# Sums of squares in a two-block fp32 kernel: four squares added by GpSimd, a reordered first product, a held PSUM bank

## The chip, the cores and the metric

The kernel runs on one core of one Trainium2 chip. The metric is the device time of one execution in microseconds, lower is better; where several executions are named, it is their median. TensorE multiplies, VectorE and ScalarE work elementwise, GpSimd is a further, slower elementwise engine, SyncE issues most of the loads.

## The reference

Activations are 512 tokens by 1024 features. Two transformer layers come first (the "first block"), then one layer of a second model (the "second block"), which also has a context stream of 256 tokens.

```python
def layer_norm(x, g, b):
    mu = jnp.mean(x, axis=-1, keepdims=True)
    var = jnp.mean(jnp.square(x - mu), axis=-1, keepdims=True)
    return (x - mu) * lax.rsqrt(var + LN_EPS) * g + b

def hybrid_layer(x, ...):                       # twice
    proj = x @ w_in                             # three kinds of attention on slices of proj
    h = layer_norm(ALPHA * x + heads @ w_o, ln1_g, ln1_b)
    ffn = (silu(h @ w_gate) * (h @ w_up)) @ w_down
    return layer_norm(ALPHA * h + ffn, ln2_g, ln2_b)

def second_block(x, c, ctx, c_ctx, ...):
    mods = split(silu(c) @ w_mod + b_mod, 9)    # and the same of c_ctx
    h = x + 0.5 * g1 * swiglu(rmsnorm(x, norm_ffn1) * (1 + sc1) + sh1, ...)
    hc = ctx + 0.5 * g1c * swiglu(rmsnorm(ctx, norm_ffn1) * (1 + sc1c) + sh1c, ...)
    ...                                         # retention, convolution, a second swiglu
```

## The kernel before, in words

Activations lie transposed, features on the 128 partitions: eight tiles of 128 features by 512 tokens, `X[:, c, :]`. Products keep fp32 accuracy by splitting: each operand is a high part and a low part, and each block product is three matmuls, high by high, high weight by low operand, low weight by high operand (`mm3`, L726 to L728). Weights come as panels of up to 16 blocks of 128 by 128, in the order of use, through two buffers (`wraw`, `whi`, `wlo`): ScalarE copies the high part (L1105), VectorE subtracts the low part (L1549), and `prep` of a panel stands in each engine's own program, mostly one panel ahead of its use (`at`). `panel` makes TensorE wait for the low part of a panel, and `two` runs a panel's tiles over all k, waiting per k for the operand's low part (`ready`), which comes after its high part.

Each engine has its own hand-ordered program, and the programs meet by semaphores. Rings hand out buffers: the PSUM banks are shared among the rings `PB` (0 to 3), `OB` (4 to 7), `AB` (0 to 6) and `ZB` (7). `take` gives the bank that was least recently handed out, whoever still reads it; the new user then waits for that reader. `hold` keeps a bank from being handed out until `give`.

A LayerNorm of the first block runs so. GpSimd adds tiles 0 to 5 of X (`add_up`, L2124), TensorE sums that and tiles 6 and 7 over the features by products with a matrix of ones (`total`, through `sum_of`, L798; each of its products is two records of the trace). VectorE subtracts the mean tile by tile (`center`, L1602, event `mid`). ScalarE squares each centred tile (`square`, L1135) into a ring of three buffers in `tmp_a` (`SQA`), and TensorE sums the eight squares by eight more products (`squares`). ScalarE turns the sum to 1/sqrt by Ln and Exp (`rstd`, L1127, L1129), then per tile VectorE scales (L1591), ScalarE adds the bias and gives the high part (`emit`, L1162), and VectorE the low part (L1572). Then the next products start: `gu f0` or `f1` after ln1, `qkB` of layer 1 after ln2 of layer 0. After ln2 of layer 1 comes the first RMS norm of the second block, rms1, whose squares ScalarE makes as it adds the LayerNorm's bias (L1361).

Between these sums TensorE makes the 36 tiles of modulation (c @ w_mod) by small products, at places written by hand (`mod_point`): "make" (L783, 16 records with 32 columns of weights), "row", a copy by ScalarE (L1117), and "turn" (L789, 4 records of two columns), which VectorE reads out (L1561). At rms1 TensorE runs the context's gate tile 0, the squares, the context's gate tile 1, the modulation, and then the x stream's gate tiles.

## Time and profile before

| | us |
|---|---|
| median of 3 executions | 3098.67 |
| lowest, highest | 3096.65, 3101.64 |
| profiled execution | 3101.29 |
| its span in the trace | 3099.5 |
| TensorE busy in the span | 3045.9 (98%) |
| VectorE, ScalarE, GpSimd busy | 1500.5, 1025.6, 277.8 |
| TensorE's mean granted clock | 0.995 |

Busy times are sums over the instructions of one engine. A matmul's duration in the trace is longer than the distance to the next one, since they are pipelined, so the distances count. Times in the rows are microseconds from the span's start. The granted clock is given as a share of 2.4 GHz; 0.50 is 1.2 GHz.

### The profile page before, as it was taken

The numbers are of one execution on the slowest core, as the hardware profiler recorded it, in microseconds if no ns is written. First come the engines' busy times: TensorE is split into PE (matmuls) and PEld (weight loads), VectorE is DVE, ScalarE is ACT, GpSimd is POOL, SyncE is SP. The second block draws the span as 40 slices with busy tenths as digits, with TensorE's granted clock in tenths as the row PEclk, the third lists the DMA queues.
The fourth block names the chain that finished last, engine by engine and source line by source line (L and its number), as shares of the span: only waits on it lengthen the run. The fifth ranks groups of instructions, "written<-read, shape, count | busy, mean of one in ns | idle before, by whom it ended". The sixth has DMA issues, their size and how long they took to land.

```text
span 3099.5 us, 35135 instructions
## 1 busy us (share of the span) xinstructions
PE 3045.9 (98%) x14888; PEld 2449.3 (79%) x14888; DVE 1500.5 (48%) x2261; ACT 1025.6 (33%) x1533; POOL 277.8 (9%) x210
## 2 busy tenths in 40 slices
PE   8999999999999999999999999999999999999998
PEld 6756778877667888878888888788888887878887
DVE  4565333344665334352323234576868694443333
ACT  4543222234543223242121123443333335232222
POOL 0232000001323000000000001010101021000000
PEclk9999999999999999999999999999999999999999
DMA  5114433222105432221212112122212123222222
GB/s 183 43 45 161 163 133 121 97 86 75 55 30 204 150 109 80 102 104 58 79 45 78 57 63 92 69 73 71 83 60 85 58 102 123 95 78 104 103 90 75
DMA packets 45051, 285.08 MB, mean 92 GB/s; under 512 B 5135, under 2 KB 5663, under 8 KB 19424
## 3 DMA queue, kind: packets, MB, share of 16 engines
q1 hardware_dynamic: 42480, 269.77, 24.5%
q0 software_dynamic: 2416, 13.09, 1.1%
q8 instruction: 117, 1.92, 0.3%
q14 instruction: 38, 0.31, 0.0%
HBM read 277.04 MB, written 5.79 MB: 91 GB/s over the span
## 4 chain that ended last, share of the span: by engine, by line
PE 93%; DVE 4%; ACT 2%; POOL 1%; issue 0%; DMA 0%; DVEq 0%; SPq 0%; POOLq 0%; ACTq 0%
PE ps L726 28%; PE ps L727 28%; PE ps L728 28%; PE ps L798 2%; PE ps L870 2%; PE ps L883 1%; PE ps L897 1%; PE ps L783 1%; ACT whi L1105 1%; DVE tmp_a L1591 0%; DVE A1l L1572 0%; DVE PP L1639 0%; PE ps L789 0%; DVE ps L1619 0%; DVE wlo L1549 0%
## 5 line engine op out<-in xcount | busy, mean ns | idle before, releaser
L726 PE MATMUL ps<-A1h,whi 128*128 128x512 f32 x2336 | 926.3, 397 | 17.5 <-DVE A1l L1568 7.8
L727 PE MATMUL ps<-A1l,whi 128*128 128x512 f32 x2336 | 912.5, 391 | 0.0
L728 PE MATMUL ps<-A1h,wlo 128*128 128x512 f32 x2336 | 912.5, 391 | 0.0
L1549 DVE TENSOR_TENSOR wlo<-wraw,whi 128x2048 fp32r<-128x2048 f32 (+2 forms) x221 | 466.1, 2109 | 258.8 <-ACT whi L1105 258.8
L1105 ACT ACTIVATE whi<-wraw 128x2048 fp32r<-128x2048 f32 (+2 forms) x221 | 385.1, 1743 | 487.8 <-PE ps L728 486.0
L726 PEld LDWEIGHTS ps<-A1h,whi 128*128 128x128 f32 x2336 | 441.1, 189 | 113.9 <-issue 19.0
L728 PEld LDWEIGHTS ps<-A1h,wlo 128*128 128x128 f32 x2336 | 440.1, 188 | 93.0
L727 PEld LDWEIGHTS ps<-A1l,whi 128*128 128x128 f32 x2336 | 440.6, 189 | 89.2 <-issue 2.2
L1727 DVE TENSOR_TENSOR SIL<-SIL,ps 128x512 f32<-128x512 f32 (+1 forms) x110 | 69.7, 634 | 583.9 <-PE ps L728 503.1
L1277 ACT ACTIVATE SIL<-ps 128x512 f32<-128x512 f32 (+1 forms) x110 | 61.0, 555 | 712.7 <-PE ps L728 712.7
L1912 DVE SCALAR_TENSOR_TENSOR CA<-YIN,vec,CA 128x512 f32<-128x512 f32 x238 | 191.2, 803 | 6.9
L726 PE MATMUL ps<-HIDMh,whi 128*128 128x512 f32 x352 | 137.1, 390 | 0.0
L727 PE MATMUL ps<-HIDMl,whi 128*128 128x512 f32 x352 | 137.1, 390 | 0.0
L726 PE MATMUL ps<-HIDh,whi 128*128 128x512 f32 x352 | 137.1, 389 | 0.0
L728 PE MATMUL ps<-HIDh,wlo 128*128 128x512 f32 x352 | 137.0, 389 | 0.0
L727 PE MATMUL ps<-HIDl,whi 128*128 128x512 f32 x352 | 137.0, 389 | 0.0
L728 PE MATMUL ps<-HIDMh,wlo 128*128 128x512 f32 x352 | 136.9, 389 | 0.0
L1177 ACT ACTIVATE PP<-ps,small 128x128 f32<-128x128 f32 (+3 forms) x128 | 67.4, 526 | 114.8 <-DVE small L1624 66.8
L726 PE MATMUL ps<-UC1h,whi 128*128 128x256 f32 x352 | 100.0, 284 | 0.0
L728 PE MATMUL ps<-UC1h,wlo 128*128 128x256 f32 x352 | 99.6, 283 | 0.0
L727 PE MATMUL ps<-UC1l,whi 128*128 128x256 f32 x352 | 99.6, 283 | 0.0
L2113 POOL TENSOR_TENSOR wlo<-wraw,whi 128x512 fp32r<-128x512 f32 (+2 forms) x70 | 95.3, 1389 | 1.8
(370 smaller groups left out, 4227.6 us busy)
## 6 DMA issues: line engine op xcount, KB each, us to landing
wraw<-wstream SPq DMA_DIRECT2D x159, 1024.0 KB, 4.8
MW<-wstream SPq DMA_DIRECT2D x36, 1024.0 KB, 5.0
wraw<-wstream SPq DMA_DIRECT2D x42, 768.0 KB, 4.3
wraw<-wstream SPq DMA_DIRECT2D x34, 640.0 KB, 3.9
wraw<-wstream SPq DMA_DIRECT2D x4, 960.0 KB, 4.7
hk<-gd POOLq DMA_DIRECT2D x1, 2560.0 KB, 13.1
X<-xT SPq DMA_DIRECT2D x4, 512.0 KB, 7.2
sx<-X POOLq DMA_DIRECT2D x1, 2048.0 KB, 7.6
```

Source lines behind the costliest of these rows:

```text
L726: mm(o, l[0], r[0], start=start, stop=False)
L727: mm(o, l[0], r[1], start=False, stop=False)
L728: return mm(o, l[1], r[0], start=False, stop=stop)
L798: last = mm(b.ap[:, 0:n], ones, src, start=i == 0, stop=i == len(parts) - 1)
L870: last = mm(b.ap[:, 0:n], q[:, 128 * i:128 * i + 128], k[:, 0:n], start=True, stop=kd != "C")
L1105: act(whi[i_ % 2][:, 0:n], wraw[i_ % 2][:, 0:n], ACT.Copy, bias=0.0, scale=1.0).then_inc(ev("hi", i_).by(act_whi), 1)
L1177: act(q.ap[:, 0:nk], b.ap[:, 0:nk], ACT.Exp, bias=nm[:, k:k + 1], scale=-1.0, accum_out=le[:, k:k + 1]).then_inc(b.free.by(act_out), 1)
L1277: act(q.ap[:, 0:n], b.ap[:, 0:n], ACT.Silu, bias=0.0, scale=1.0).then_inc(q.full.by(act_out), 1)
L1549: tt(wlo[i_ % 2][:, 0:n], wraw[i_ % 2][:, 0:n], raw(whi[i_ % 2][:, 0:n]), SUB).then_inc(ev("lo", i_).by(dve_wlo), 1)
L1727: tt(q.ap[:, 0:n], q.ap[:, 0:n], b.ap if n == 512 else b.ap[:, 256:512], MUL).then_inc(b.free.by(dve_out), 1)
L1912: stt(out=to, in0=y.ap[:, k:k + 512], scalar=v("convw", CONV_W * c + k), in1=o.ap, op0=MUL, op1=ADD).then_inc(ev("tap", c, k).by(dve_out), 1)
L2113: last = tt(wlo[i % 2][:, part], wraw[i % 2][:, part], raw(whi[i % 2][:, part]), SUB)
```

## The change

Five sums of squares are changed: ln1 and ln2 of both layers, and rms1.

- Squares go to a buffer of eight tiles, `SQL`, instead of the ring of three. GpSimd adds squares 0 to 3 (rms1: 0 to 5) into tile 0 (`add_late`). TensorE sums squares 4 to 7 and then that sum (rms1: that sum, then 6 and 7), in `late_squares`.
- The PSUM bank of the LayerNorm's total is held until the squares' sum has its own.
- ScalarE squares tile 0 before it copies the first modulation row, and tiles 1 and 2 before the second.
- In `two` with `early`, TensorE waits per k for the operand's high part, runs the two products that need only that for all tiles, then waits for the low part. This is used for the first panel of f0, f1, f2 (x stream) and of qkB in layer 1.
- At rms1 both context gate tiles run ahead of the squares' sum.
- Around qkB of layer 1 the last turn of modulation moves behind the first panel, and VectorE's readout of the turns before it moves behind the split of the second panel.

```diff
+        SQL = sb("SQL", [128, 8, 512], T0)
...
-        mod_point(("ln2", 0, 1), 2, index["qkB", 1, 0], last=True)
+        mod_point(("ln2", 0, 1), 2, index["qkB", 1, 0])
+        mod_point(("qkB", 1), 0, index["qkB", 1, 0], last=True)
...
-            def two(p, op, tiles, names, ring=PB, k0=0, group=0):
+            def two(p, op, tiles, names, ring=PB, k0=0, group=0, early=False):
+
                 bs = [ring.take(*n) for n in names]
-                for k in range(p.nk):
+                for k in range(p.nk if early else 0):
+                    e.wait_ge(ev("high", op.name, k, group))
+                    r = op.at(k)
+                    for b, t in zip(bs, tiles):
+                        if k == 0:
+                            e.wait_ge(b.before)
+                        w = p.block(k, t)
+                        mm(b.ap, w[0], r[0], start=k == 0, stop=False)
+                        mm(b.ap, w[1], r[0], start=False, stop=False)
+                    e.wait_ge(ready(op, k, group))
+                    for b, t in zip(bs, tiles):
+                        last = mm(b.ap, p.block(k, t)[0], r[1], start=False, stop=k == p.nk - 1)
+                        if k == p.nk - 1:
+                            last.then_inc(b.full.by(product), 1)
+                for k in range(0 if early else p.nk):
...
-            def total(key, acc, src, made):
+            def total(key, acc, src, made, keep=False):
+                if keep:
+                    OB.hold("total", *key)
...
+            def late_squares(key, n, parts):
+
+                sum_of(OB, ("sq sum",) + key, 512,
+                       [(SQL[:, 0, :], ev("sq acc", *key, n - 1), None) if c is None else (SQL[:, c, :], ev("sq", *key, c), None) for c in parts])
...
-                    two(p, op, (0, 1), [("gate", name, tag, j), ("up", name, tag, j)])
+                    two(p, op, (0, 1), [("gate", name, tag, j), ("up", name, tag, j)], early=j == 0 and name != "f3")
...
-                    two(panel("qkB", l, n), opIn[l], (0, 1), [("qkB", l, n, 0), ("qkB", l, n, 1)])
+                    two(panel("qkB", l, n), opIn[l], (0, 1), [("qkB", l, n, 0), ("qkB", l, n, 1)], early=l > 0 and n == 0)
+                    if l and n == 0:
+                        mods("qkB", 1)
...
-                total(("ln1", l), TA[:, 3, :], X, lambda c: ev("x", "wo", l, c))
+                total(("ln1", l), TA[:, 3, :], X, lambda c: ev("x", "wo", l, c), keep=True)
                 mods("ln1", l, 0)
-                squares(OB, SQA, ("ln1", l), 512, 8)
+                late_squares(("ln1", l), 4, (4, 5, 6, 7, None))
+                OB.give("total", "ln1", l)
                 mods("ln1", l, 1)
...
             gates("f2", "c", opC, 0)
-            squares(OB, SQA, ("rms1",), 512, 8)
             gates("f2", "c", opC, 1)
+            late_squares(("rms1",), 6, (None, 6, 7))
             mods("rms1")
...
+            def late_square(key, c, made):
+
+                e.wait_ge(made)
+                act(SQL[:, c, :], X[:, c, :], ACT.Square, bias=0.0, scale=1.0).then_inc(ev("sq", *key, c).by(act_out), 1)
...
-                mods("ln1", l, 0)
                 for c in range(8):
-                    square(SQA, ("ln1", l), c, X[:, c, :], ev("mid", "ln1", l, c))
+                    late_square(("ln1", l), c, ev("mid", "ln1", l, c))
+                    if c in (0, 2):
+                        mods("ln1", l, 0, part=c // 2)
...
                     at("qkB", l, n)
+                    if l and n == 0:
+                        mods("ln2", 0, 1)
...
+                    if l and n:
+                        mods("qkB", 1)
...
                     emit(X, opIn[1], TA, ("ln2", l), 512, lambda c: v("ln", 32 * l + 16 + c), lambda c: v("ln", 32 * l + 24 + c), ())
-                    mods("ln2", l, 1)
...
+            def add_late(key, n):
+
+                for c in range(1, n):
+                    e.wait_ge(ev("sq", *key, 0) if c == 1 else ev("sq acc", *key, c - 1), ev("sq", *key, c))
+                    tt(SQL[:, 0, :], SQL[:, 0, :], SQL[:, c, :], ADD).then_inc(ev("sq acc", *key, c).by(pool_out), 1)
...
+                add_late(("ln1", l), 4)
                 restore(opN[l], ("ln1", l))
...
+            add_late(("rms1",), 6)
```

ln2 and rms1 are changed in the same way as ln1 where the diff is cut.

## Rows read from the trace of the kernel before

**Rows 1.** The page's chain that ended last, share of the span by engine.

```profile
PE 93%; DVE 4%; ACT 2%; POOL 1%; issue 0%; DMA 0%; DVEq 0%; SPq 0%; POOLq 0%; ACTq 0%
```

**Rows 2.** Waits of PE, whole span: waited for, us in total, times, longest.

```profile
PE ps L726 <- DVE A1l L1572: 7.1, 5, 3.9
...
PE ps L726 <- DVE wlo L1549: 4.5, 4, 2.0
```

**Rows 3.** Timeline, ln1 of layer 0: start us, us, engine line op, [idle before <-releaser].

```profile
279.66 4.87 DVE L1602 SCALAR_TENSOR_TENSOR X<-ps,X 128x512 f32<-128x512 f32 x8 [2.79 <-PE ps L798]
...
281.55 0.38 ACT L1117 ACTIVATE mrow<-ps 128x256 f32<-128x256 f32 x1 [0.48 <-PE ps L783]
...
281.83 1.66 ACT L1135 ACTIVATE tmp_a<-X 128x512 f32<-128x512 f32 x3
...
282.50 7.13 PE L798 MATMUL ps<-tmp_a,mats 128*128 128x512 f32 x16 [0.49 <-ACT tmp_a L1135]
...
289.68 0.69 ACT L1127 ACTIVATE tmp_a<-ps,small 128x512 f32<-128x512 f32 x1 [1.89 <-PE ps L798]
...
291.85 1.39 ACT L1162 ACTIVATE A1h<-tmp_a,vec 128x512 fp32r<-128x512 f32 x2 [0.55 <-DVE tmp_a L1591]
...
293.50 0.47 PE L726 MATMUL ps<-A1h,whi 128*128 128x512 f32 x1 [0.79 <-DVE A1l L1572]
...
307.02 0.50 PE L726 MATMUL ps<-A1h,whi 128*128 128x512 f32 x1 [0.81 <-DVE wlo L1549]
```

**Rows 4.** Timeline, ln2 of layer 0 and the first panels of layer 1.

```profile
679.88 10.13 PE L798 MATMUL ps<-tmp_a,mats 128*128 128x512 f32 x16 [1.89 <-DVE X L1602]
...
702.47 0.85 DVE L1561 TENSOR_SCALAR small<-ps,vec 128x2 f32<-128x2 f32 x6
...
706.14 0.50 PE L726 MATMUL ps<-A1h,whi 128*128 128x512 f32 x1 [0.53 <-DVE wlo L1549]
```

**Rows 5.** Timeline, ln1 of layer 1 and its second panel.

```profile
958.00 7.13 PE L798 MATMUL ps<-tmp_a,mats 128*128 128x512 f32 x16 [0.48 <-ACT tmp_a L1135]
...
969.00 0.54 PE L726 MATMUL ps<-A1h,whi 128*128 128x512 f32 x1 [0.79 <-DVE A1l L1572]
...
983.14 0.48 PE L726 MATMUL ps<-A1h,whi 128*128 128x512 f32 x1
```

**Rows 6.** Timeline, ln2 of layer 1 and rms1.

```profile
1349.81 7.13 PE L798 MATMUL ps<-tmp_a,mats 128*128 128x512 f32 x16 [0.48 <-ACT tmp_a L1135]
...
1351.58 2.28 DVE L1549 TENSOR_TENSOR wlo<-wraw,whi 128x2048 fp32r<-128x2048 f32 x1
...
1359.88 0.36 PE L726 MATMUL ps<-UC1h,whi 128*128 128x256 f32 x1
...
1365.71 8.02 PE L798 MATMUL ps<-tmp_a,mats 128*128 128x512 f32 x16
...
1380.55 0.38 ACT L1117 ACTIVATE mrow<-ps 128x256 f32<-128x256 f32 x1 [5.42 <-PE ps L783]
...
1382.99 0.48 PE L726 MATMUL ps<-A1h,whi 128*128 128x512 f32 x1
```

**Rows 7.** GpSimd's additions, TensorE's sums: duration ns min/median/max, first and last start, forms.

```profile
L798 PE MATMUL ps<-tmp_a,mats x112: 379/592/1219, 137.1 to 1920.3; 128*128 128x512 f32 x106, 128*128 128x256 f32 x6
...
L2124 POOL TENSOR_TENSOR tmp_a<-tmp_a,X x16: 1276/1298/3158, 269.3 to 1338.4; 128x512 f32<-128x512 f32 x16
```

**Rows 8.** Windows: us, busy of PE, PEld, DVE, ACT, POOL, granted clock, DMA share, GB/s.

```profile
679.20:685.90 6.70, 6.02 (x7) 2.50 (x8) 1.13 (x6) 1.95 (x4) 0.00 (x0) 0.50 0.52 218
...
969.30:972.70 3.40, 3.40 (x9) 2.63 (x8) 3.40 (x6) 1.95 (x3) 0.00 (x0) 0.50 0.85 325
...
846.30:849.70 3.40, 3.40 (x10) 1.46 (x9) 3.40 (x14) 2.14 (x7) 0.00 (x0) 0.51 0.80 287
```

**Rows 9.** Timeline of PE in the attention of layers 0 and 1.

```profile
171.24 0.30 PE L883 MATMUL ps<-mats,PP 128*128 128x128 f32 x1 [2.44 <-DVE PP L1639]
...
845.96 0.30 PE L883 MATMUL ps<-mats,PP 128*128 128x128 f32 x1 [2.45 <-DVE PP L1639]
```

More of the change, by code:

```diff
@@ L997, in tensor @@
                     ffn("f0", [("x", opN[l], opHid[l])], 11)
-                total(("ln2", l), TA[:, 3, :], X, lambda c: ev("x", f"f{l}", 3, c))
+                total(("ln2", l), TA[:, 3, :], X, lambda c: ev("x", f"f{l}", 3, c), keep=True)
                 mods("ln2", l, 0)
-                squares(OB, SQA, ("ln2", l), 512, 8)
+                late_squares(("ln2", l), 4, (4, 5, 6, 7, None))
+                OB.give("total", "ln2", l)
                 mods("ln2", l, 1)
             gates("f2", "c", opC, 0)
-            squares(OB, SQA, ("rms1",), 512, 8)
             gates("f2", "c", opC, 1)
+            late_squares(("rms1",), 6, (None, 6, 7))
             mods("rms1")
@@ L1350, in scalar @@
                     at("gu", "f2", 0)
-                mods("ln2", l, 0)
                 for c in range(8):
-                    square(SQA, ("ln2", l), c, X[:, c, :], ev("mid", "ln2", l, c))
+                    late_square(("ln2", l), c, ev("mid", "ln2", l, c))
+                    if c in (0, 2):
+                        mods("ln2", l, 0, part=c // 2)
                 rstd(OB.of("sq sum", "ln2", l), TA[:, 3, :], 512, 1024, eps5, ("ln2", l), OB.of("total", "ln2", l).full)
@@ L1361, in scalar @@
                 act(X[:, c, :], X[:, c, :], ACT.Identity, bias=v("ln", 32 + 24 + c), scale=1.0).then_inc(ev("x", "ln2", 1, c).by(act_out), 1)
-                square(SQA, ("rms1",), c, X[:, c, :], ev("x", "ln2", 1, c))
+                late_square(("rms1",), c, ev("x", "ln2", 1, c))
             rstd(OB.of("sq sum", "rms1"), TA[:, 3, :], 512, 1024, eps6, ("rms1",), ev("rs", "ln2", 1))
@@ L2152, in gpsimd @@
                 add_up(TA[:, 3, :], X, ("ln2", l), lambda c: ev("x", f"f{l}", 3, c), ev("rs", "c1") if l else ev("rs", "ln1", l))
+                add_late(("ln2", l), 4)
                 if l + 1 < DEPTH:
                     restore(opIn[1], ("ln2", l))
+            add_late(("rms1",), 6)
             for first, n in ((1, 2), (2, 4), (4, 6)):
```

## The prediction, made before the changed kernel ran

> **What bounds the kernel now.** I read the chain that ended last first: TensorE holds 93% of it [rows 1]. So only two things can shorten the span: less TensorE work, or shorter waits of TensorE. The view of TensorE's waits gives the second [rows 2]: the waits that touch the change are those on the low halves of an operand (7.1 us in five places), on the low half of a weight panel (4.5 us in four); a third stands in the rows of ln2, 1.89 us on a centred tile [rows 4]. Then I read the stretch around each normalisation in order of time [rows 3 to 6]. There TensorE does not do model products; it adds squares up by products with a matrix of ones. Eight of them are sixteen records in 7.13 us [rows 3]; that time less a record's length of 0.59 [rows 7], by fifteen steps, is 0.436 us a step, 0.87 us for one product. Last I read the granted clock of the short stretches in which it stands at 0.50, and waits that ended with it or without it [rows 8, 9].
>
> **The change part by part.** Five sums of squares lose products: 3 of 8 at ln1 and ln2 of both layers, 5 of 8 at rms1. That removes 17 products, 14.8 us of TensorE work; each site is worked out by itself, because the wait ahead of the sum grows.
>
> *ln1 of layer 0* [rows 3]. Now the squares start on ScalarE at 281.83, after both copies of modulation rows, and TensorE starts at 282.50. In the new order the first square needs only the first centred tile: VectorE's eight tiles take 4.87 us from 279.66, 0.61 each, so it can start at 280.4. Squares follow every 0.52 us (three in 1.66), a row copy adds 0.28 (281.55 to 281.83). Square 0 at 280.4, row, squares 1 and 2 at 281.2 and 281.7, row at 282.25 (its products are ready, as the row at 281.55 shows), squares 3 and 4 at 282.55 and 283.05, the latter done at 283.7. TensorE now begins with square 4, at 283.75, which is 1.25 us later than now, and needs 7.13 - 3 x 0.87 = 4.5 us: done at 288.25, not 289.63. Gain 1.4 us. Squares 0 to 3 become one operand by three additions on GpSimd of 1.30 us each [rows 7], from 281.9, some 1.4 us apart: done at 286.1. TensorE wants the sum as its fifth operand at 287.2, so 1.1 us covers them; without that cover each later microsecond is lost in full. The statistic, ScalarE's normalised tiles and the next panel's split follow from the end of the sum, all 1.4 us earlier.
>
> *High parts ahead of low.* The first product can start when the high tile is there, up to 0.79 us earlier, the wait for the low tile at 293.50 [rows 3]. I cost this at nothing. The second weight panel is split by ScalarE and VectorE only behind the eight normalised tiles, and TensorE already waits 0.81 us for it at 307.02. What starts earlier ahead of it waits longer at it: 1.6 us. The same holds in ln2 of layer 0, with 0.53 us at 706.14 [rows 4]; at rms1 another wait is later than the low part (below). Bounds: 0 to 0.79 a site. I take 0.
>
> *ln2 of layer 0* [rows 4]. TensorE is done with its modulation products at 677.99 and waits until 679.88 for VectorE's last centred tile: the sum's PSUM bank is the one in which VectorE still reads the total. With the total's bank held the sum takes another, and the wait left is square 4, by the same steps 679.05. Then 4.5 us: 683.55, where it now takes 10.13 from 679.88, to 690.01. Gain 6.45. Of this 3.0 is clock: 10.13 against 7.13 for the same sixteen records. In exchange VectorE's readout of modulation turns is put behind the split of the second panel, and one of those banks is wanted by that panel's first tile: two of the six instructions of 0.85 us, 0.3 us. The turn moved behind the first panel costs 0.6 us of TensorE in a wait of 1.5 us, so nothing. Gain 6.15.
>
> *ln1 of layer 1.* As layer 0, 1.4 us, and the half-clock stretch at 969.30 [rows 8] follows here on a 0.79 us wait [rows 5]: the second panel starts at 983.14, while layer 0's 307.02 and the distance of 675.50 between the two sums (282.50 and 958.00 [rows 5]) would give 982.52. With that 0.6, 2.0 us.
>
> *ln2 of layer 1* [rows 6]. Squares start at 1350.4 instead of 1349.81 and end at 1354.9 instead of 1356.94: 2.0 us. Here VectorE splits a panel at 1351.58, for 2.28 us, right in GpSimd's additions. A GpSimd addition takes 1.30 us at the median and 3.16 at most in this trace [rows 7]. If the third is caught in full it comes at 1355.2, not 1352.7, 1.4 us too late; if not, nothing. I take 0.2, so 1.8 us. The Trainium skill, SBUF — State Buffer, section Who interferes with whom, says that VectorE with two SBUF inputs and GpSimd lock each other out of a shared port for a whole instruction; that longest addition agrees, and by the rule the cost would be one of my two ends, whichever starts first.
>
> *rms1* [rows 6]. Now the context tile 0 runs from 1359.88 to 1365.71, 5.83 us, then the sum takes 8.02 us (0.9 more than at ln1, waiting for squares), then tile 1, and the first product of the x stream is at 1382.99. ScalarE waits 5.42 us for a modulation row that stands behind tile 1, and holds the first normalised tile back. New: both tiles end at 1371.5, three products (six records, 2.8 us) at 1374.3; the five additions go beside the 5.8 us of tile 1. Then the modulation products. The last turn needs a row that ScalarE copies only behind two normalised tiles: from the statistic to the first of them 2.17 us (289.68 to 291.85), two take 1.39 [rows 3], the row 0.4, the turn 0.6, so the x stream can start at 1378.9. Gain 4.1 us. TensorE waits about 1.1 us there that it doesn't wait now.
>
> **The sum**: 1.4 + 6.15 + 2.0 + 1.8 + 4.1 = 15.45 us. From the profiled execution's own 3101.29 us (span 3099.5) that is 3085.8, if the clock holds everywhere that is changed.
>
> **What is late next: the clock.** The changed sites trade work for waits, ahead of and behind small products: 1.7 us at ln1 twice (282.01 to 283.75; now 0.5), 1.05 at ln2 twice (1.89 and 0.48 now), 1.6 twice and 1.5 once ahead of the second panels (0.81 at most now), 1.1 at rms1. The clock is not indifferent to such waits. It stands at 0.50, the lower of its two levels (1.2 GHz), over 3.4 us from 969.30 behind a wait of 0.79 us [rows 5, 8], while the same wait at 293.50 costs nothing [rows 3]; it stands so from 846.30 behind a wait of 2.45 us, while the same wait of 2.44 us at 171.24 costs nothing [rows 8, 9]. At 679.20 it lasts 6.7 us. So the same wait falls in one execution and not in another; a fall costs half of its length, 1.7 or 3.4 us. Eight waits, none longer than these: I take four falls of 1.7, so 6.8 us, and 3092.6. The profiled execution lies 2.6 us above the median of 3098.67, and its three falls outside the change need not come again; I take 1.0 off for that: **3091.6 us**, 7.1 below the median, 0.23%.
>
> **The rivals.**
> *No fall where the waits are this short*: 3085.8 less 1.0, 3084.8. For it: the 2.44 us at 171.24, and the waits of 0.8 us at 293.50 and 307.02, all without a fall. Against it: 969.30. The Trainium skill, TensorE: Matmul & The Clock Gate, section HAM oscillation — how this bites in real kernels, warns only of idle gaps longer than any that this change makes; by that rule this rival is the result. The fall at 969.30 disagrees. Chance 0.25 (with two falls or fewer).
> *Most of the eight waits fall*: 3084.8 + 7 x 1.7 = 3096.7, no change that can be told. For it: products of a few columns stand ahead of each of them, as at 969.30. Chance 0.16.
> *GpSimd is late*, that is, the change moves the work but doesn't free TensorE: if all three additions take 3.16 us they end 9.5 us from 281.9, at 291.4, and the sum at 292.3, 2.7 later than now, at four sites. That gives 3084.8 + 16.2 = 3101.0, and it decides once the additions take over 1.7 us each (1.1 us of cover). Against it: seen beside VectorE's work out of PSUM they take 1.30. Chance 0.04.
> *Slower*: falls of the long kind, 3.4 us each as at 679.20, because the wait itself lies in the fallen stretch and TensorE doesn't come back in one. Place: ahead of the sums at ln1 and ln2, and at rms1, five, and three ordinary ones at the panels: 17.0 + 5.1 = 22.1, so 3106.9. It decides from four long ones beside four ordinary (20.4 us). Chance 0.05.
> The forecast keeps 0.50, from three to six falls.
>
> **How the numbers follow.** A measurement of this kernel can tell about 0.2%, 6.2 us, from no change: faster is below 3092.5. The forecast's own range, 3 to 6 falls, is 3089.9 to 3095.0, about 0.6 of it faster: 0.30; with the first rival 0.55. Within 0.2%: 0.20, most of the seven-fall case, part of the GpSimd case: 0.39. Slower 0.06. The range reaches from 3084 (no falls, and some of the 0.79 us of the early start) to 3098 (all eight).
>
> **What would show it.** Right: sums of ten and six records in 4.5 and 2.8 us; the sum at ln2 of layer 0 starting 0.8 us earlier, no wait on VectorE's centred tile; waits on the panel split near 1.6 us; clock at 0.50 near some changed sites, never gone. Wrong: a sum waiting on GpSimd; first products earlier and the second panel earlier by more than the sum's end; or a clock of 1.00 throughout the changed sites.

## The result, and the profile after

The changed kernel takes 3091.14 us, median of 17 runs (3088.75 to 3097.19), the kernel before beside it 3098.22 (3094.72 to 3103.12): a ratio of 0.9977, 95% interval 0.997 to 0.9985. That is 0.23% faster, little but clear of the noise. The prediction was 3091.6.

The page of the changed kernel, its parts 1 and 4 (busy us and instructions of TensorE; the chain that ended last) and, below, TensorE's waits (waited for, us in total, times, longest):

```profile
span 3087.9 us, 35073 instructions
...
PE 3029.5 (98%) x14854; PEld 2444.0 (79%) x14854; DVE 1502.2 (49%) x2261; ACT 1023.2 (33%) x1533; POOL 300.4 (10%) x227
...
PE 92%; DVE 4%; ACT 2%; POOL 1%; issue 0%; DMA 0%; DVEq 0%; SPq 0%; POOLq 0%; ACTq 0%
```

```profile
PE ps L728 <- DVE wlo L1584: 6.4, 4, 2.0
PE ps L815 <- ACT SQL L1176: 5.3, 4, 1.7
PE ps L728 <- DVE A1l L1607: 5.5, 3, 3.9
```

TensorE still holds the chain, as in [rows 1]. The waits changed as foretold: those on the low half of an operand went from 7.1 us to 5.5 [rows 2], those on a panel's low half from 4.5 to 6.4, and 5.3 us now stand ahead of the four sums of ln1 and ln2, where there were 3.3 (0.49, 1.89, 0.48 and 0.48, [rows 3 to 6]). The list has no wait on GpSimd's additions of squares; the waits on GpSimd in it, 1.0 us ahead of the totals and 0.8 us at a later sum, were there before.

The timeline of ln1 of layer 0 (start us, us, engine line op, [idle before <-releaser]), which answers to [rows 3]:

```profile
279.91 0.63 ACT L1176 ACTIVATE SQL<-X 128x512 f32<-128x512 f32 x1 [10.41 <-DVE X L1637]
...
281.47 3.98 POOL L2175 TENSOR_TENSOR SQL<-SQL 128x512 f32<-128x512 f32 x3 [5.22 <-ACT SQL L1176]
...
282.01 2.71 ACT L1176 ACTIVATE SQL<-X 128x512 f32<-128x512 f32 x5
...
283.21 4.56 PE L815 MATMUL ps<-SQL,mats 128*128 128x512 f32 x10 [1.66 <-ACT SQL L1176]
...
305.13 0.50 PE L728 MATMUL ps<-A1h,whi 128*128 128x512 f32 x1 [1.64 <-DVE wlo L1584]
```

Ten records in 4.56 us, begun behind a wait of 1.66; three additions on GpSimd are done at 285.45, before TensorE wants their sum as its fifth operand; and 1.64 us of waiting ahead of the second panel, where there were 0.81. I compare a site by the distance from its first record of totals to its second panel: here 276.30 to 305.13, 28.83 us, against 30.24 before. At ln2 of layer 0 the totals begin so in the kernel before (its sum and second panel are in [rows 4]):

```profile
672.18 1.02 PE L798 MATMUL ps<-tmp_a,mats 128*128 128x512 f32 x2
```

and in the changed kernel the totals, the sum and the second panel:

```profile
671.94 1.02 PE L815 MATMUL ps<-tmp_a,mats 128*128 128x512 f32 x2
...
678.75 4.56 PE L815 MATMUL ps<-SQL,mats 128*128 128x512 f32 x10 [1.00 <-ACT SQL L1176]
...
699.78 0.47 PE L728 MATMUL ps<-A1h,whi 128*128 128x512 f32 x1 [1.94 <-DVE small L1596]
```

The table puts each site's prediction beside that distance (at the last, the distance from the totals of ln2 to the first x product):

| site | before, us | after, us | gain | predicted |
|---|---|---|---|---|
| ln1 layer 0 | 30.24 | 28.83 | 1.41 | 1.4 |
| ln2 layer 0 | 33.96 | 27.84 | 6.12 | 6.15 |
| ln1 layer 1 | 30.86 | 28.85 | 2.01 | 2.0 |
| ln2 layer 1 and rms1 | 39.48 | 33.99 | 5.49 | 5.9 |

The gains add up to 15.0 us. Of these 3.6 are falls of the clock that lay on two sites in the one profile of the kernel before (3.0 at ln2 of layer 0, 0.6 at ln1 of layer 1) and on none of these distances in the one profile after, so 11.4 us are work and waits. A second profile of the changed kernel (the first experiment) has 27.85, 28.85 and 33.99 us at the last three sites, so these distances repeat; at the first it has 30.53, 1.70 more, with a fall of 3.4 us on the sum.

Where the missing 0.4 us of the last row went, the timeline of TensorE at rms1 shows, which answers to [rows 6]:

```profile
1361.87 2.74 PE L815 MATMUL ps<-SQL,mats 128*128 128x512 f32 x6
...
1368.62 0.58 PE L806 MATMUL ps<-vec,mrow 128*128 128x2 f32 x4 [0.93 <-ACT mrow L1145]
1369.96 0.50 PE L750 MATMUL ps<-A1h,whi 128*128 128x512 f32 x1 [0.77 <-DVE small L1596]
```

The wait of 0.93 us for the last row was foreseen. The 0.77 us behind it was not: the first x tile takes a bank out of which VectorE still reads a modulation turn.

**The clock.** Each execution's record has its span and its mean granted clock. A "fall" is a stretch in which the granted clock stands at half. So (1 - clock) x span is half of the time that falls lay on, which is their price where TensorE works all through. The clock is given to 0.001, that is 3 us, so only means over several executions are used. What is left, "the rest", is work and waits. A fall that lies in a wait is counted though it costs nothing, so the rest is too small. In every profile some 3.3 us of the falls lie behind TensorE's last product (it ends at 3078.43 in the changed kernel, and the clock stands at half from 3081.4 to the end), and up to the experiment that fills the longest wait another 3.4 us lie at that wait, where they cost nothing either. The rest of the kernel before is 3084.5 to 3085.5 us on the four chips of the experiments, so rests can be compared across chips to about 1 us.

```
kernel                        executions  mean span  falls  rest
before                            58        3097.5    12.5  3085.0
changed                           17        3089.9    16.5  3073.3
changed, again                     8        3088.6    15.4  3073.1
high parts not early               5        3087.7    15.4  3072.3
panel split ahead                  5        3081.3    14.2  3067.1
waits filled                       5        3087.5    12.4  3075.2
split ahead, not early             6        3089.1    19.6  3069.5
bank held only (of before)        11        3095.7    11.5  3084.2
eight products                    11        3097.5    15.8  3081.7
sum between tiles                 11        3092.9    14.9  3078.0
split ahead, sums filled           5        3080.7    11.7  3069.0
split ahead, long wait filled      5        3078.8     8.6  3070.1
split ahead, rms1 earlier          5        3080.8    14.8  3066.0
all that helped                    5        3077.3     7.4  3070.0
```

By this table the change took 11.7 us of work and waits away, beside 11.4 in the traces, and added 4.0 us of falls. The split is not sharp: from one execution of a kernel to the next, a microsecond more of falls goes with a span only about 0.6 us longer (17 executions of the changed kernel, 58 of the kernel before), and the executions whose clock is given as 0.996 differ by 10.1 us (3097.5, ten of them, and 3087.4, seven). The prediction had 11.85 (15.45 less the 3.6 us of falls that it took out of ln2 of layer 0 and ln1 of layer 1) and 6.8 - 3.6 = 3.2.

### The profile page after: what moved, and what is told of

Read it like the earlier page. It is cut to its first block, busy times and chain, and to the rows that moved or that the text cites. A ratio compares the mean times of both kernels' runs of the same rounds, so it can differ in the third digit from the quotient of the medians.

```text
span 3087.9 us, 35073 instructions
## 1 busy us (share of the span) xinstructions
PE 3029.5 (98%) x14854; PEld 2444.0 (79%) x14854; DVE 1502.2 (49%) x2261; ACT 1023.2 (33%) x1533; POOL 300.4 (10%) x227
## 4 chain that ended last, share of the span: by engine, by line
PE 92%; DVE 4%; ACT 2%; POOL 1%; issue 0%; DMA 0%; DVEq 0%; SPq 0%; POOLq 0%; ACTq 0%
PE ps L728 28%; PE ps L730 28%; PE ps L729 28%; PE ps L815 2%; PE ps L894 2%; PE ps L907 1%; PE ps L921 1%; DVE tmp_a L1626 1%; DVE A1l L1607 1%; PE ps L800 1%; POOL tmp_a L2162 1%; ACT whi L1133 0%; DVE wlo L1584 0%; ACT SQL L1176 0%; DVE ps L1654 0%
## 5 line engine op out<-in xcount | busy, mean ns | idle before, releaser
L728 PE MATMUL ps<-A1h,whi 128*128 128x512 f32 x2272 | 901.8, 397 | 19.4 <-DVE A1l L1603 7.5
L730 PE MATMUL ps<-A1h,wlo 128*128 128x512 f32 x2272 | 888.3, 391 | 0.0
L729 PE MATMUL ps<-A1l,whi 128*128 128x512 f32 x2272 | 888.2, 391 | 0.0
L728 PEld LDWEIGHTS ps<-A1h,whi 128*128 128x128 f32 x2272 | 429.3, 189 | 112.5 <-issue 17.0
L730 PEld LDWEIGHTS ps<-A1h,wlo 128*128 128x128 f32 x2272 | 428.4, 189 | 90.7
L729 PEld LDWEIGHTS ps<-A1l,whi 128*128 128x128 f32 x2272 | 429.1, 189 | 87.2 <-issue 2.2
```

Of the source, the lines that this page charges most:

```text
L728: mm(o, l[0], r[0], start=start, stop=False)
L729: mm(o, l[0], r[1], start=False, stop=False)
L730: return mm(o, l[1], r[0], start=False, stop=stop)
```

## The experiments

The theory: the gain is TensorE's products taken away and the sum of squares ended earlier; the early high parts are worth nothing as long as the second panel's split is late; the new waits let the clock fall. Rivals: the early start earns the gain; the order or the buffers do; falls have nothing to do with the waits.

**The changed kernel again**, as a control on the same chip as the next two and as the first experiment on waits filled.

> The changed kernel, nothing edited, as the control beside the three other kernels: 3091 us, ratio to the kernel before 0.9977 (0.997 to 0.9985). Any edit below is judged against this one, with about 2 us as what can be told apart.

3090.23 us, ratio 0.9971 (0.9961 to 0.9981). Its profile shows falls at other places than the first one did, inside the sum of squares of ln1 and on its second panel. I name a fall by the start of the window of 1.7 us in which it begins, here 283.9 and 307.7.

```profile
283.90:287.30 3.40, 3.40 (x5) 1.38 (x6) 1.08 (x4) 1.49 (x3) 2.13 (x2) 0.54 1.00 417
307.70:311.10 3.40, 3.40 (x10) 2.63 (x10) 2.53 (x5) 2.70 (x3) 3.40 (x3) 0.55 1.00 412
```

(Windows, columns as in [rows 8]: the granted clock is 0.54 and 0.55.) So one profile doesn't tell where a kernel's falls are, only where they can be.

**The early high parts taken back.**

```diff
-                    two(p, op, (0, 1), [("gate", name, tag, j), ("up", name, tag, j)], early=j == 0 and name != "f3")
+                    two(p, op, (0, 1), [("gate", name, tag, j), ("up", name, tag, j)])
...
-                    two(panel("qkB", l, n), opIn[l], (0, 1), [("qkB", l, n, 0), ("qkB", l, n, 1)], early=l > 0 and n == 0)
+                    two(panel("qkB", l, n), opIn[l], (0, 1), [("qkB", l, n, 0), ("qkB", l, n, 1)])
```

> The changed kernel without its new order in the first products: every first panel waits for both parts of a chunk again. Theory (the early high parts only move the wait to the second panel, where ScalarE and VectorE are late with the weights' split): the records of the second panel come within 0.3 us of the changed kernel at ln1 layer 0 and layer 1 and at ln2 layer 0, the waits of 1.6 to 1.9 us ahead of it vanish and as much stands ahead of the first panel instead; 3091 us, within 2 us. Rival (the early start itself earned the gain): each of three places loses 0.8 to 1.6 us, time 3094 to 3096 us, near the kernel before.

3088.23 us, 0.9965 (0.9951 to 0.9979), so not slower than the control; the rest is 3072.3 against 3073.1, at the same 15.4 us of falls. The rival, 3094 to 3096 us, fails. In the trace the first panel waits again:

```profile
292.67 0.49 PE L728 MATMUL ps<-A1h,whi 128*128 128x512 f32 x1 [0.78 <-DVE A1l L1607]
...
306.79 0.48 PE L728 MATMUL ps<-A1h,whi 128*128 128x512 f32 x1
```

The second panel starts 29.45 us behind the totals, 0.62 later than in the changed kernel, although a fall of 1.7 us lies on the first panel in this profile (from 292.4) and 0.78 of wait ahead of it. My expectation of 0.3 us was for a clock that holds: about 1.9 us of the 2.5 went into the wait for the split that stood there.

**The second panel's split moved ahead** of the squares on ScalarE and of the normalised rows on VectorE.

```diff
 # ScalarE, ahead of the squares of ln1
+                at("gu", f"f{l}", 0)
 # ScalarE, ahead of the squares of ln2 of layer 0
+                else:
+                    at("qkB", 1, 0)
 # VectorE, behind mods("ln1", l, 0)
+                at("gu", f"f{l}", 0)
 # VectorE, behind mods("ln2", 0, 0)
+                    at("qkB", 1, 0)
```

> The changed kernel with the split of the second panel's weights moved ahead of the squares on ScalarE and ahead of the normalised rows on VectorE, at ln1 of both layers and ln2 of layer 0. Theory (the second panel's wait of 1.6, 1.7 and 1.9 us is for that split alone): these three waits go, 5.2 us, and of the clock falls beside them two at 1.7 us each; ScalarE is then up to 1 us later with the first square, which comes back in the wait ahead of the sum: net 3084 to 3088 us. Rival (the split is work that the two engines have no room for, and the squares and rows are late by as much): the wait moves ahead of the sum or of the first panel, 3091 us within 2 us. Rival 2 (the split ahead of the squares costs more than it gives, because two engines of the chain wait for the panel's landing): 3093 us or more.

3083.79 us, 0.9947 (0.9935 to 0.996). The timeline of TensorE at ln1 of layer 0:

```profile
275.92 1.13 PE L815 MATMUL ps<-tmp_a,mats 128*128 128x512 f32 x2 [0.65 <-POOL tmp_a L2167]
...
282.83 4.56 PE L815 MATMUL ps<-SQL,mats 128*128 128x512 f32 x10 [1.66 <-ACT SQL L1176]
...
302.98 0.48 PE L728 MATMUL ps<-A1h,whi 128*128 128x512 f32 x1
```

27.06 us where the changed kernel has 28.83, and the wait ahead of the sum is 1.66 as before: ScalarE and VectorE were idle ahead of the squares and of the rows (10.41 and 4.88 us in the changed kernel), so the split fitted in at no cost. The rest falls by 6.0, against 5.2 us of waits. At ln2 of layer 0 the wait on VectorE's readout of turns went with it, because the readout no longer stands behind the split.

**The same, with the early high parts taken back.** The edit is that of the second experiment.

> The kernel with the panel split moved ahead (3083.8 us), with the new order in the first products taken back. Theory (the early start is worth nothing only while the second panel is late; with that panel ready each of three first panels that starts 0.8 us later ends 0.8 us later): 3086.2 us, 2.4 above, with waits of 0.8 us at three first panels and none at the second. Rival (the early start is worth nothing anywhere): 3083.8 us, and a wait shows up elsewhere in place of it.

3090.69 us, 0.9971 (0.9959 to 0.9983): 7 us over the split alone, not 2.4. (The two ran on different chips; each ratio is to the kernel before on its own chip.) The rest says 2.4 (3069.5 against 3067.1), as the theory had it; the other 5.4 are falls (19.6 against 14.2). With the panel ready no wait behind them hides a fall. At the changed sites of layers 0 and 1 this profile has falls at 290.7, 676.6, 686.8, 952.0 and 962.2: the sums of ln2 of layer 0 and ln1 of layer 1, and all three first panels, which stand behind a wait of 0.78. So the early start is worth nothing beside a late split. Beside one in time it is worth 2.4 us of waits, as foretold, and some 5 us more of falls, which rest on five and six executions and on one profile of each.

**The bank of the total held, nothing else, on the kernel before.**

```diff
+                OB.hold("total", "ln1", l)
                 total(("ln1", l), TA[:, 3, :], X, lambda c: ev("x", "wo", l, c))
                 mods("ln1", l, 0)
                 squares(OB, SQA, ("ln1", l), 512, 8)
+                OB.give("total", "ln1", l)
 # and the same at ln2
```

> The kernel before with one edit: the total's bank is held until the sum of squares has taken another one. Theory (at ln2 of layer 0 the 1.89 us wait on the last centred tile is for that bank): the sum of squares there starts with its first square, 0.8 to 1.4 us earlier, with sixteen records as before, and nothing changes at the other sums; 1 us below the kernel before, 3097.5, and with the clock fall at that place gone up to 1.7 us more, 3096. Rival (the wait is for the tile's own data or for nothing that holding changes): 3098.5 us and the wait still there.

3097.53 us, 0.9993 (0.9984 to 1.0002). By time alone nothing can be told; the trace settles it:

```profile
678.10 2.41 PE L798 MATMUL ps<-tmp_a,mats 128*128 128x512 f32 x5 [0.48 <-ACT tmp_a L1139]
```

With its totals at 671.80 the sum starts 6.30 us behind them, where it took 7.70 (672.18 to 679.88 [rows 4]), and the wait is for the first square, not for VectorE's last tile. So the bank was what the sum waited for. Held alone it moves the start by 1.4 us; in the changed kernel, where the wait for square 4 takes its place, 0.9 us of that is left.

**All eight squares summed by TensorE**, the additions on GpSimd gone.

```diff
-[(SQL[:, 0, :], ev("sq acc", *key, n - 1), None) if c is None else (SQL[:, c, :], ev("sq", *key, c), None) for c in parts]
+[(SQL[:, c, :], ev("sq", *key, c), None) for c in range(8)]
...
-                for c in range(1, n):
+                for c in range(0):
```

> The changed kernel with all eight squares summed by TensorE from their own tiles again, and no addition on GpSimd. Theory (the gain is TensorE work taken away): the sum starts with the first square, some 1.6 us earlier, and takes 7.13 us, not 4.56, so it ends 0.9 to 1.2 us later at four sites; at rms1 it takes 7.1 us, not 2.74, which adds 4.4. Together 8 to 9 us, less up to 2 us for waits ahead of the sum that are gone with their clock falls: 3096 to 3100 us, near the kernel before. Rival (what earned the gain was keeping the squares apart and the order of the rest): 3091 us, within 2.

3099.28 us, 1.0000 (0.9991 to 1.0009): by time the gain is gone. A sum looks so:

```profile
282.04 7.11 PE L815 MATMUL ps<-SQL,mats 128*128 128x512 f32 x16
```

It starts 5.11 us behind the totals, not 6.91, and ends at 12.22 rather than 11.47; at rms1 ten records more cost 4.4. The rest is 8.6 us higher than the control's, which I had at 8 to 9. By the distances of the table this kernel is 8.6 us behind the changed one too (0.75, 1.42, 0.75 and 5.71 at the four rows). So the products removed are 8.6 of the 11.4 us. The other 2.8 come from the buffers, the order and the held bank, which this kernel keeps: its rest is still 3.2 us below that of the kernel before on this chip. In time they don't show, because falls are 15.8 us against 12.6.

**The sum of rms1 put back between the context tiles.**

```diff
             gates("f2", "c", opC, 0)
+            late_squares(("rms1",), 6, (None, 6, 7))
             gates("f2", "c", opC, 1)
-            late_squares(("rms1",), 6, (None, 6, 7))
```

> The changed kernel with the sum of rms1 put back between the two context tiles. Theory (both tiles ahead of the sum are cover for five additions on GpSimd and for the squares): TensorE waits 1.5 to 4 us for the added sum behind tile 0, and ScalarE's modulation row comes late behind tile 1 again; the x stream starts 2 to 4 us later, 3093 to 3095 us. Rival (the order there is neutral, the gain of rms1 is only the five products less): the x stream starts within 1 us of the changed kernel, 3091 us.

3093.16 us, 0.9984 (0.9975 to 0.9993); the rest is 4.9 us higher.

```profile
1352.91 7.36 POOL L2175 TENSOR_TENSOR SQL<-SQL 128x512 f32<-128x512 f32 x5 [8.02 <-ACT SQL L1176]
...
1360.32 4.54 PE L815 MATMUL ps<-SQL,mats 128*128 128x512 f32 x6 [4.17 <-POOL SQL L2175]
```

One tile of 5.8 us can't cover squares and five additions; TensorE waits 4.17 us for GpSimd, and the six records take 4.54 us instead of 2.74 because a fall lies on them in this profile. The second tile is the cover, as the prediction had it.

**Waits filled.** Products whose result is overwritten, put into waits of TensorE. Every `fill(bank, n)` is n products of the matrix of ones with the constant tile.

```diff
+            def fill(b, n):
+                e.wait_ge(b.before, ev("mats"))
+                for _ in range(n):
+                    mm(b.ap, ones, mats[:, :], start=True, stop=True)
...
             def late_squares(key, n, parts):
+                fill(OB.take("sq sum", *key), {"ln1": 2, "ln2": 1, "rms1": 0}[key[0]])
 # and 2 into the first bank of the second panel, at ln1 and at ln2 of layer 0
```

> The changed kernel with products added that compute nothing that is used: two ahead of the sum of squares at ln1, one at ln2, and two ahead of the second panel at ln1 of both layers and ln2 of layer 0, each 0.43 us or 0.87 us of TensorE in a stretch where it waits 1.0 to 1.9 us. They end before the wait would have, so the place of the sum and of the panel is the same. Theory (a wait costs its own length and about 1.7 us more where the granted clock falls to 0.50 behind it): the falls at the changed places are gone and the time is 3 to 6 us lower, 3085 to 3088 us, with more products. Rival (falls come from elsewhere, not from these waits): 3091 us within 2 us, or up to 3 us more where a filler outlasts its wait.

3089.28 us, 0.9968 (0.9955 to 0.998). Falls went down, 12.4 from 15.4, but the rest went up by 2.1. The trace has one place for it, ln2 of layer 0, whose second panel starts 29.97 us behind the totals and not 27.84:

```profile
698.06 3.22 PE L836 MATMUL ps<-mats 128*128 128x512 f32 x4 [1.86 <-DVE small L1605]
```

The wait there was for a bank that VectorE reads, and the filler wants the same bank: it starts when the wait is over, and is pure loss: 1.74 us at full clock by the price of a filler below, more here, where a fall lies on it.

> The kernel with the panel split moved ahead (3083.8 us) with products that compute nothing that is used ahead of the sum of squares: two at ln1, one at ln2, 0.87 and 0.43 us in waits of 1.66 and 1.00. The place of the sum stays. Theory (the wait ahead of the sum is what lets the granted clock fall there, in about half of the sites): one to three falls fewer at 1.7 us, ratio to the kernel before 0.9930 to 0.9942. Rival (these falls come with the execution and not with the waits that this fills): the same as without, 0.9947 within 0.0006.

This one fills only ahead of the sums, on top of the split moved ahead: 3083.03 us, 0.995 (0.9938 to 0.9962), no better than without. I had the price of a filler wrong (0.87 us each, two records, so two fill the 1.66 whole), which does no harm here. The falls do react: the kernels with a wait of 1.66 or 1.00 ahead of the sum (the changed one, its control, and six more) have eleven falls at 32 such sums in their profiles; the three that fill them have none at 12 (the last experiment below is one of them). If filling changed nothing and each sum were a draw of its own, all eleven would lie at the 32 with a chance of 1.7%. The sums of one profile are not quite independent, so the evidence is weaker than that. Yet the mean falls drop by 2.5 us and the rest rises by 1.9. Most of such a rise the traces don't show (span less falls is 3067.7 us in this profile, 3066.9 in that with the split alone). The mean spans, 3081.3 and 3080.7, differ by 0.6 us, so what the fillers are worth in time stays open, between 0 and 2.5 us.

**The longest wait filled**: behind the last sum before the last feed-forward block TensorE waits 3.86 us, and the clock stood at half over 6.8 us from inside that wait in every profile up to here.

```diff
             square_total(("ffn2",), TD[:, 3, :], SQD)
+            fill(PB.take("gate", "f3", "x", 0), 8)
             ffn("f3", [("x", opX3, hidM3)])
```

> The kernel with the panel split moved ahead, with eight products that compute nothing that is used behind the last sum before the last feed-forward block. There TensorE waits 3.86 us in every execution, and the granted clock stands at 0.50 from inside that wait for 6.8 us, 5.3 of them in work. The fillers are 3.5 us, inside the wait. Theory (a fall follows from a TensorE that waits): no fall there in the profile, and the panel behind it ends 2.6 us earlier; ratio to the kernel before 0.9938, against 0.9947. Rival (a fall comes from something else at that place, such as the load of three engines): the fall is there as before and the time the same.

3081.28 us, 0.9943 (0.9929 to 0.9957). Windows over that wait and the panel behind it, first of the kernel with the split ahead alone, then with the filler:

```profile
2703.00:2709.70 6.70, 2.91 (x8) 0.94 (x6) 3.00 (x5) 3.33 (x5) 0.00 (x0) 0.92 0.00 1
2709.70:2716.50 6.80, 6.74 (x18) 5.33 (x19) 6.80 (x11) 3.61 (x5) 0.00 (x0) 0.58 0.00 0
```

```profile
2698.00:2707.00 9.00, 9.00 (x24) 4.20 (x23) 4.75 (x7) 4.07 (x6) 0.00 (x0) 1.00 0.00 1
2707.00:2716.00 9.00, 9.00 (x39) 6.95 (x38) 6.87 (x11) 6.39 (x7) 0.00 (x0) 1.00 0.00 0
```

The fall is gone, with VectorE and ScalarE loaded as before, and it is gone in the last experiment too, after twelve profiles of kernels without this filler that all have it: it follows from TensorE's wait. But eight fillers are 7.03 us, not 3.5: the first panel starts 9.1 us behind the sum instead of 6.65, and ends where it had ended with the fall. My expectation of 2.6 us earlier fails on the fillers' price.

**The last row and the readouts at rms1 moved one tile earlier.**

```diff
-                    if point and c in (0, 2):
-                        mods(*point, part=c // 2)
+                    if point and c in (0, 1 if point == ("rms1",) else 2):
+                        mods(*point, part=min(c, 1))
...
-                    if beside and c == 3:
+                    if beside and c == (2 if key == ("rms1",) else 3):
```

> The kernel with the panel split moved ahead, and at rms1 the last modulation row copied by ScalarE behind one normalised tile rather than two, and the six readouts by VectorE one tile earlier. Theory (the x stream starts 1.3 us behind its first high tile because of the last row, 0.9, and of a bank that VectorE still reads, 0.4 to 0.8): the first x product comes 0.7 to 0.9 us earlier, as counted from the sum of rms1; ratio to the kernel before 0.9944. With the fall that stands there in most executions gone, 0.9939. Rival (the next tile is late instead, because VectorE reads the turns ahead of it): the first product is earlier and the panel ends where it did, 0.9947.

3082.47 us, 0.995 (0.9938 to 0.9963); the time can't tell. In the trace the first x product comes 6.77 us behind the start of the sum of rms1, not 8.09, and a wait of 0.41 us on a gate's bank is new behind that panel:

```profile
1359.18 2.74 PE L815 MATMUL ps<-SQL,mats 128*128 128x512 f32 x6
...
1365.95 0.50 PE L750 MATMUL ps<-A1h,whi 128*128 128x512 f32 x1
...
1378.21 0.50 PE L728 MATMUL ps<-A1h,whi 128*128 128x512 f32 x1 [0.41 <-DVE SIL L1765]
```

So 0.9 of 1.3 us are left, and the rest is 1.1 lower.

**All that helped**: the split ahead, rms1 earlier, fillers at the sums, four at the long wait, two at the first value panel of the first retention head.

> What the experiments point to, in one kernel: the panel split moved ahead, the rms1 row and readouts earlier, and products that compute nothing that is used in four kinds of wait, each now sized by what the fillers measured (0.87 us each): two ahead of the sum at ln1 (wait 1.66), one at ln2 (1.0), four behind the last sum before the last feed-forward block (3.86, where eight outlasted the wait by 2.4 us), two at the first value panel of the first retention head (1.99). Theory (each wait that is filled keeps its clock; fillers inside a wait cost nothing): no falls near the four sums, near 1945 and near 2710; against the kernel with the split alone 2.6 us for the last block, 1.7 for the value panel, 0.9 for rms1 and about 2 for the sums, 7 us together: ratio to the kernel before 0.9925, 3076 us. Rival (falls that are avoided at one place come at another): ratio 0.9935 to 0.9947, with as much half clock in the profile as in the others, 12 to 15 us.

3079.42 us, 0.9933 (0.9919 to 0.9946): faster than both kernels, and short of the 0.9925 forecast. Falls are 7.4 us in the mean, about half of the 14.2 with the split alone, so they don't move elsewhere; but the rest is 3070.0, not 3066. The mean span is 4.0 us shorter than with the split alone, where 7 were forecast. The largest part of the shortfall:

```profile
2693.93 2.79 PE L815 MATMUL ps<-tmp_d,mats 128*128 128x512 f32 x6
2696.57 3.60 PE L836 MATMUL ps<-mats 128*128 128x512 f32 x8
2700.59 0.47 PE L728 MATMUL ps<-A1h,whi 128*128 128x512 f32 x1 [0.43 <-DVE A1l L1618]
2714.10 0.50 PE L728 MATMUL ps<-A1h,whi 128*128 128x512 f32 x1 [2.37 <-DVE wlo L1595]
```

Four fillers keep the first panel where it was and its clock whole. It ends 2.4 us earlier, and TensorE then waits 2.37 us for the second panel's split, which starts behind the eight rows (VectorE at 2711.75). The second panel starts 20.17 us behind the start of the sum, as it did with the fall (20.16 in the control): that fall had cost nothing. Its 3.4 us are in the falls of every row of the table but this one and that of the longest wait filled, and never in the span. That is most of the difference between 3070.0 and 3066, and 2.6 us of the forecast were for it. The split moved ahead there too would be the next thing; it wasn't tried.

## Why the prediction was right

**The sums** were sized right. Square 4 was put 1.25 us later than the old start, it came 1.19 later (6.91 against 5.72 us behind the totals), and ten records took 4.56, not 4.5. Additions on GpSimd run 1.33 us apart, not 1.4. The experiment with eight products shows the 17 products to be the cause of 8.6 of the 11.4 us.

**High parts ahead of low** at nothing: right, and for the reason given. The wait at the second panel is 1.64 us, foretold 1.6; taking the early start back changed nothing, and the split moved ahead gave it a price. What the prediction left out is that the late split is itself the next gain: 6.0 us from four calls of `at`.

**ln2 of layer 0**: 6.12 against 6.15. The sum starts 6.81 us behind the totals (678.75 to 671.94) instead of 7.70, so 0.89 earlier, foretold 0.83, and takes 4.56 instead of 10.13, of which 3.0 is clock; together 6.46. These 3.0 are luck of the profile, not the change's: the kernel with the bank alone has no fall on that sum, and the second experiment has one on it with the change in. The 0.3 us for VectorE's readout behind the split is right too: the wait at that panel is named after the readout and is 1.94, where 1.5 was foretold.

**ln2 of layer 1**: 2.06 us from the totals to the first context tile (16.37 to 14.31) against 1.8. GpSimd's additions weren't held up, VectorE was:

```profile
1341.03 3.97 POOL L2175 TENSOR_TENSOR SQL<-SQL 128x512 f32<-128x512 f32 x3 [8.84 <-ACT SQL L1176]
...
1344.04 3.11 DVE L1584 TENSOR_TENSOR wlo<-wraw,whi 128x2048 fp32r<-128x2048 f32 x1
```

3.11 us where the same split took 2.28 [rows 6], while the three additions took their ordinary 1.3 each. The third addition had begun at 1343.73, 0.31 us ahead of the split, and ended at 1345.00. The longest addition of the kernel before, 3.16 us from 270.70, is the reverse case: there a split ran from 270.03 to 272.72. In both the one that began second paid. The Trainium skill, SBUF — State Buffer, section Who interferes with whom, has whoever issues first keep the port and the other wait, and both cases agree. Here VectorE had the time: it stood idle for 1.61 us behind the split. So that the additions were not late depended on the third being ahead of the split by 0.31 us, and the prediction's 0.2 us for this was the price of a risk, not a sizing. The rival in which GpSimd is late had its price and place right only for one tile of cover: with the sum between the tiles it waits 4.17 us.

**rms1** is the one term that was mis-sized: 3.43 us (23.11 to 19.68), not 4.1. The step counted the last row and not the bank: 0.77 us for a turn that VectorE reads out behind its third row. From the end of the sum to the first x product it had 4.6 us, and the changed kernel takes 5.35. The same kind of wait was counted at ln2 of layer 0 and overlooked here.

**The clock.** Four falls of 1.7 were forecast in the changed sites. The changed kernel's profile has three, its control's four; in the means falls rose by 4.0 us where 3.2 followed from the text. So the size was right, and so was the spread: the two profiles of one kernel differ by 3.4 us in falls. That the time came within 0.5 us is luck all the same. The profiled execution stood 2.6 us above the median and 1.0 was taken off for that by judgement, and the terms are known to a microsecond or two at best (10.1 to 11.7 us for work and waits, against 11.85). The rival without falls (3084.8) leaned on a rule of the Trainium skill, TensorE: Matmul & The Clock Gate, section HAM oscillation — how this bites in real kernels; the runs speak against using it as a bound, with falls behind waits of 0.78, 1.00 and 1.66 us. The same page of the Trainium skill, section A second HAM failure mode: psum-queue depth-cycling, has a kernel in which small idle stretches between groups of products do it, by coming often. The traces here agree in that short idle stretches are enough; whether their number matters no run here shows. The slower rival (falls that cost 3.4 each) didn't come in the changed kernel's two profiles; of the profiles of the experiments one has such a fall at a changed site, at rms1 from 1363.4, with the split ahead.

## What to carry to other kernels

Where an operand's wait is removed, look at what the next panel waits for before pricing it: the early start was worth nothing until the late split behind it was moved, and 2.4 us of waits after, with some 5 us of falls beside them. A product that only adds squares up costs as much TensorE time as any other of its kind (0.87 us here), and GpSimd, where it is idle and its work is covered, can take it over: TensorE never waited for it with two tiles of cover, and 4.17 us with one. Compare executions by span and clock together, and then look in the trace: the clock's share went from 7.4 to 19.6 us between these kernels, the rest showed effects that the medians hid, and the distances in the traces showed where the rest itself misleads, since it subtracts falls that cost nothing.

## What the runs showed of the hardware that I had not expected

- A fall costs nothing where TensorE will wait soon after. At the last feed-forward block 6.8 us of half clock were in every profile of a kernel that doesn't fill the wait, and removing them left the second panel at 20.17 us behind the sum, against 20.16.
- A second short wait of TensorE seems likelier to bring a fall close behind another: the two kernels with waits of 0.78 us at the first panels behind waits of 1.66 and 1.00 at the sums show five falls each at the same five places of ln1 of layer 0, ln2 of layer 0 and ln1 of layer 1 (292.4, 678.3, 688.5, 953.7, 963.9 and 290.7, 676.6, 686.8, 952.0, 962.2). Waits of 0.8 us stand at the first panels of ln1 in the kernel before and in that with the bank held too, behind waits of 0.48 us at the sums, and there the first profile has one fall at such a place, at 969.0, and the second has none. So this is a pattern from few profiles, and no more.
- A product of 128 x 128 by 128 x 512 in plain f32 is two records and 0.87 us here; eight of them took 7.03.
- Where a split on VectorE (both inputs in SBUF) and an addition on GpSimd overlap, the one that began second was stretched: the split to 3.11 us from 2.28, the addition to 3.16 from 1.30.
